# A product-key expert layer: the dense sum over all experts' V rows replaced by gathers of the chosen rows

## What is computed

```python
e = (i1 * PEER_NKEYS + i2).reshape(T, PEER_HEADS * PEER_TOPK)
gate = jax.nn.softmax(cv, axis=-1).reshape(T, PEER_HEADS * PEER_TOPK)
act = jax.nn.gelu(jnp.einsum('ted,td->te', u_tab[e], xb).astype(jnp.float32))
coef = (gate * act).astype(xb.dtype)
return jnp.einsum('te,ted->td', coef, v_tab[e])
```

## Time and profile before

| What | Value |
|---|---|
| median of three runs | 5477.62 us |
| span of the profiled execution | 5473.6 us |
| PE busy | 5015.2 us, 92% of the span |
| DVE busy | 2899.3 us, 53% |
| ACT busy | 1068.2 us, 20% |
| POOL busy | 455.4 us, 8% |
| moved by DMA | 476.12 MB, mean 87 GB/s |

### The profile page before, as it was taken

The page is one execution under the profiler, slowest core; times in us unless marked ns, Lnnn a source line. Parts: engine busy times, 40 slices in busy tenths (PEclk is TensorE's granted clock), DMA queues, the critical chain, the costliest instruction groups (busy, mean ns, idle before and its releaser), DMA issues. The chain is left out here.

```text
span 5473.6 us, 76074 instructions
## 1 busy us (share of the span) xinstructions
PE 5015.2 (92%) x26871; PEld 4496.7 (82%) x26871; DVE 2899.3 (53%) x7212; ACT 1068.2 (20%) x1825; POOL 455.4 (8%) x328
## 2 busy tenths in 40 slices
PE   7999889998798999988887699999999999999996
PEld 6757888884598999988887688888888899889886
DVE  1021733333315999877776566666644444444444
ACT  2111111111311222222222211111111121112111
POOL 0000033430000000000000022222200000000000
PEclk9999589999799999999989899999999999999998
DMA  3100300002222233244445533333321221121122
GB/s 114 39 23 16 129 23 1 1 1 85 96 70 79 100 105 110 77 134 131 136 131 144 154 141 140 142 142 133 141 76 57 72 72 59 61 72 64 56 72 81
DMA packets 450919, 476.12 MB, mean 87 GB/s; under 512 B 311344, under 2 KB 376240, under 8 KB 449328
## 3 DMA queue, kind: packets, MB, share of 16 engines
q1 hardware_dynamic: 136240, 354.12, 18.6%
q10 hardware_dynamic: 307728, 91.43, 6.2%
q0 software_dynamic: 6768, 28.32, 1.4%
HBM read 336.45 MB, written 137.36 MB: 87 GB/s over the span
## 5 line engine op out<-in xcount | busy, mean ns | idle before, releaser
L1752 DVE TENSOR_TENSOR peer_y<-peer_y,stored_pv 128x512 f32<-128x512 f32 x648 | 443.0, 686 | 271.1 <-PE stored_pv L1781 270.3
L1779 PE MATMUL stored_pv<-stored_Vh,stored_Ch 128*128 128x512 f32 x1296 | 505.5, 390 | 33.1 <-DVE stored_Cl L1738 33.1
L1780 PE MATMUL stored_pv<-stored_Vl,stored_Ch 128*128 128x512 f32 x1296 | 505.2, 390 | 0.0
L1781 PE MATMUL stored_pv<-stored_Vh,stored_Cl 128*128 128x512 f32 x1296 | 505.1, 390 | 0.0
L1952 DVE TENSOR_TENSOR peer_y<-peer_y,experts_pv 128x512 f32<-128x512 f32 x504 | 341.8, 687 | 286.1 <-PE experts_pv L1992 286.1
L1975 PE MATMUL experts_pu<-peer_xh,experts_Uh 128*128 128x384 f32 x1344 | 450.5, 335 | 7.0 <-DVE experts_Ul L1918 7.0
L1977 PE MATMUL experts_pu<-peer_xh,experts_Ul 128*128 128x384 f32 x1344 | 450.2, 335 | 0.0
L1976 PE MATMUL experts_pu<-peer_xl,experts_Uh 128*128 128x384 f32 x1344 | 450.2, 335 | 0.0
L1990 PE MATMUL experts_pv<-experts_Vh,experts_Ch 128*128 128x512 f32 x1008 | 396.1, 393 | 15.1 <-DVE peer_y L1952 12.7
L1599 DVE TENSOR_SCALAR gates_scaled<-gates_iota,retrieve_slotT 128x128 f32<-128x128 f32 x1152 | 396.2, 344 | 0.0
L1991 PE MATMUL experts_pv<-experts_Vl,experts_Ch 128*128 128x512 f32 x1008 | 393.7, 391 | 0.0
(11 more groups left out here) (297 smaller groups left out, 9408.9 us busy)
## 6 DMA issues: line engine op xcount, KB each, us to landing
gates<-gates_G ACTq DMA_DIRECT2D x72, 1024.0 KB, 11.0
stored_C<-acts SPq DMA_DIRECT2D x72, 576.0 KB, 3.8
stored_G<-gates SPq DMA_DIRECT2D x72, 576.0 KB, 4.8
stored_Vr<-in_peer_v SPq DMA_DIRECT2D x72, 512.0 KB, 6.4
experts_G<-gates SPq DMA_DIRECT2D x56, 576.0 KB, 3.8
experts_Ur<-in_peer_u SPq DMA_DIRECT2D x56, 512.0 KB, 5.7
experts_Vr<-in_peer_v SPq DMA_DIRECT2D x56, 512.0 KB, 5.9
acts<-topk_act SPq DMA_DIRECT2D x135, 192.0 KB, 1.9
```

The lines of the kernel that those rows point to most:

```text
L1752: nc.vector.tensor_tensor(dst, dst, pv[r % RING][:], ALU.add).then_inc(y_added, 1)
L1779: mm(pv[r % RING][:], Ch[p][j][:, t], Vh[p][j][:, cols], start=(j == 0), stop=False)
L1780: mm(pv[r % RING][:], Ch[p][j][:, t], Vl[p][j][:, cols], start=False, stop=False)
L1781: last = mm(pv[r % RING][:], Cl[p][j][:, t], Vh[p][j][:, cols], start=False, stop=(j == 1))
```

## The change

The Gelu values of all 128 blocks are now made in topk (6 blocks a tile, 54 in all) and in a new stage rest (74 blocks, U products only), and stored to DRAM. They go to nine tensors `acts0` to `acts8`, one per tile of tokens, in which the value of expert e and token t is cell 128 e + t. The stages gates, stored and experts are removed. A new stage values computes from `slotT` the expert number `row` and the cell number `cell` of each token's 128 slots. Per token POOL then issues two indirect DMAs: one brings the 128 Gelu values into a column of `act`, one brings the 128 rows of V (4 KB each) into one of 16 buffers, a row per partition. DVE multiplies the values of a tile by their weights and writes them to a matrix W that is zero elsewhere; PE multiplies W (128 slots x 32 columns, one of which is not zero) by the token's V rows, in plain float32, and sums 32 tokens into 32 partitions of PSUM. Four tokens are handled in turn, each in its own group of 32 columns of the PE array. ACT copies a finished tile to `y`.

The diff, cut to what the prediction speaks of (removed stages are printed above):

```diff
 class Ahead:
     def store(self, sp, n):
         for c in range(NTC):
             sp.wait_ge(self.gelu_done, 3 * n + (c + 4))
-            sp.dma_start(self.dram["acts"][n + self.first][:, c * TC:(c + 1) * TC], self.act[c][:]).then_inc(self.act_out[c], 16)
+            for t in range(TC // P):
+                dst = self.dram[f"cells{c * (TC // P) + t}"][n + self.first]
+                sp.dma_start(dst, self.act[c][:, t * P:(t + 1) * P]).then_inc(self.act_out[c], 16)
...
-TOPK_AHEAD = 5
-GATE_AHEAD = 3
+TOPK_AHEAD = 6
...
-                    if half == 0:
-                        ahead.low(dve, t * A + 4, 4)
+                    ahead.low(dve, t * A + 4 + half, 4 + half)
...
+def stage_rest(core, xh, xl, first):
+    R = 2
+    LEFT = P - first
...
+        def _(sp):
+            ahead.load(sp, 0)
+            with sp.Fori(0, LEFT // R - 1) as i:
+                for b in range(R):
+                    ahead.load(sp, i * R + (b + 1))
+                    ahead.store(sp, i * R + b)
...
+        def _(pe):
+            ahead.begin(pe=pe)
+            with pe.Fori(0, LEFT // R) as i:
+                for b in range(R):
+                    for c in range(NTC):
+                        ahead.products(pe, i * R + b, b, c)
...
+def stage_values(core, y):
+    Q = 4
+    QW = P // Q
+    RING = 16
...
+        def _(pool):
+            def gather_act(i, t):
+                pool.indirect_dma_start(act[i % 2][:, t:t + 1], None, dram[f"acts{i}"],
+                                        bass.IndirectOffsetOnAxis(ap=cell[:, i * P + t:i * P + t + 1], axis=0))\
+                    .then_inc(act_in[i % 2], 16)
+
+            def gather_row(i, m, j):
+                n = (i * QW + m) * Q + j
+                if n >= RING:
+                    pool.wait_ge(v_used, (n - RING) // Q + 1)
+                t = i * P + j * QW + m
+                pool.indirect_dma_start(V[n % RING][:], None, dram["peer_v"],
+                                        bass.IndirectOffsetOnAxis(ap=row[:, t:t + 1], axis=0)).then_inc(v_in[n % RING], 16)
...
+            for t in range(P):
+                gather_act(0, t)
+            pool.wait_ge(rows_made, 1)
+            for i in range(TILES):
+                if i >= 1 and i + 1 < TILES:
+                    pool.wait_ge(coef_done, i)
+                for m in range(QW):
+                    for j in range(Q):
+                        if i + 1 < TILES:
+                            gather_act(i + 1, m * Q + j)
+                        gather_row(i, m, j)
...
+        def _(pe):
+            for i in range(TILES):
+                pe.wait_ge(coef_done, i + 1)
+                if i >= 2:
+                    pe.wait_ge(tile_read, i - 1)
+                for m in range(QW):
+                    n = (i * QW + m) * Q
+                    for half in range(2):
+                        for j in range(Q):
+                            if half == 0:
+                                pe.wait_ge(v_in[(n + j) % RING], 16 * ((n + j) // RING + 1))
+                            last = nc.tensor.matmul(py[i % 2][j * QW:(j + 1) * QW, half, :], W[i % 2][:, j, m * QW:(m + 1) * QW],
+                                                    V[(n + j) % RING][:, half * HW:(half + 1) * HW],
+                                                    start=(m == 0), stop=(m == QW - 1))
+                    last.then_inc(v_used, 1)
...
                 stage_topk(core, xh, xl)
-                stage_gates(core, xh, xl)
+                stage_rest(core, xh, xl, TILES * TOPK_AHEAD)
             y = pr.sb("y", [P, TILES, D])
-            made = TILES * (TOPK_AHEAD + GATE_AHEAD)
-            stage_stored(core, y, made)
-            stage_experts(core, xh, xl, y, made)
+            stage_values(core, y)
             stage_final(core, y)
```

More of the change, by code:

```diff
@@ L1552, in _ @@
             turn(TILES - 1)
-def stage_gates(core, xh, xl):
-    nc, dram = core.nc, core.dram
[L1561 to L1578, removed]
+def stage_rest(core, xh, xl, first):
+    nc = core.nc
+    R = 2
+    LEFT = P - first
+    with Stage(core, "rest") as st:
+        ahead = Ahead(core, st, R, first, xh, xl)
+        block = st.block()
+        @block.sync
+        def _(sp):
[4 more added lines that the diff above has]
+                    ahead.store(sp, i * R + b)
+            ahead.load(sp, LEFT - 1)
+            ahead.store(sp, LEFT - 2)
+            ahead.store(sp, LEFT - 1)
+            ahead.stored(sp, LEFT)
+        @block.scalar
+        def _(act):
+            ahead.begin(act=act)
+            ahead.high(act, 0, 0)
+            with act.Fori(0, LEFT // R - 1) as i:
+                for b in range(R):
+                    ahead.high(act, i * R + (b + 1), (b + 1) % R)
+                    ahead.gelu(act, i * R + b)
+            ahead.high(act, LEFT - 1, 1)
+            ahead.gelu(act, LEFT - 2)
+            ahead.gelu(act, LEFT - 1)
+        @block.vector
+        def _(dve):
+            ahead.begin(dve=dve)
+            with dve.Fori(0, LEFT // R) as i:
+                for b in range(R):
+                    ahead.low(dve, i * R + b, b)
+        @block.tensor
+        def _(pe):
+            ahead.begin(pe=pe)
+            with pe.Fori(0, LEFT // R) as i:
+                for b in range(R):
+                    for c in range(NTC):
+                        ahead.products(pe, i * R + b, b, c)
@@ new lines, in stage_values @@
+def stage_values(core, y):
+    nc, dram = core.nc, core.dram
+    Q = 4
+    QW = P // Q
+    RING = 16
+    with Stage(core, "values") as st:
+        tok = st.sb("tok", [P, TILES, P])
+        expert = st.sb("expert", [P, T])
+        row = st.sb("row", [P, T], U32)
+        cell = st.sb("cell", [P, T], U32)
+        act = [st.sb(f"act{i}", [P, P]) for i in range(2)]
+        W = [st.sb(f"W{i}", [P, Q, QW * QW]) for i in range(2)]
+        V = [st.sb(f"V{i}", [P, D]) for i in range(RING)]
+        py = [st.psum(f"py{i}", [P, 2, HW]) for i in range(2)]
+        tok_done = st.sem("tok_done")
+        w_zero = st.sem("w_zero")
+        ch = st.sem("chain")
+        cells_made, rows_made = st.sem("cells_made"), st.sem("rows_made")
+        act_in = [st.sem(f"act_in{i}") for i in range(2)]
+        v_in = [st.sem(f"v_in{i}") for i in range(RING)]
+        coef_done = st.sem("coef_done")
+        v_used = st.sem("v_used")
+        tile_made = st.sem("tile_made")
+        tile_read = st.sem("tile_read")
@@ L1586, in _ @@
         @block.vector
         def _(dve):
[L1588 to L1600, removed]
+            link = Chain(dve, ch)
@@ L1602, in _ @@
         @block.tensor
         def _(pe):
[L1604 to L1617, removed]
@@ L1619, in _ @@
-        @block.scalar
[L1620 to L1649, removed]
```

349 lines of the change are left out of this document (41 added, 308 removed).

## The result

The changed kernel takes 6659.34 us (median of four runs, 6656.88 to 6660.9) against 5477.17 us before: 1.216 times as long, 95% interval 1.2145 to 1.2179. The forecast of 5897 us had the sign right; the time lies inside the range, close to its upper end, and the loss is 1182 us where 419 us were forecast. The new stage, values, takes some 3260 us in place of 2506 us; everything else came out as summed.

The account below looks back on a forecast made before the run. PE was taken to set the old kernel's pace, and POOL's gathers that of values. 5473.6 - 3133 + 113 + 933, 3391 us against the median, plus 2506 us for values gave 5897 us, 7.7% slower; range 5220 to 6700 us.

Parts of the forecast that it names:

- the sixth block: Topk: a sixth block of U products per tile makes PE the longer side by some 12 us, +113 us over 9 tiles.
- the 74 blocks left over: Rest: 74 blocks at 12.47 us are 923 us, plus 10 us for first load and split, +933 us.
- their cover: Rest: a 7.3 us chain of stores, load and split hides behind a 12.47 us block; 90 us if cover were gone.
- That the gathers decide: Values: POOL's two gathers a token, 2.16 us, are slowest and hide the DMA engines' 1.56 us and PE's 0.43 us.
- the first rival: Values: gathers near the plain 0.54 us, so DMA engines bind at 1.56 us a token; 5277 us, 3.7% faster; chance 0.32.
- The price of a gather: Values: twice a plain DMA's 0.54 us on POOL, 1.08 us for each of 2304 gathers, giving a stage of 2506 us.
- Rival 2: Values: POOL reads index after index or waits for data; 8939 us at 2.4 us a gather; chance 0.10, extreme 0.02 of it.
- Rival 3: Values: PE's column groups run serially, 1.72 us a token; 5462 to 5503 us, or 7512 us at half clock; chances 0.04, 0.03.
- The DMA engines' 1.56 us a token: Values: 1.42 us for a token's V rows plus 0.14 us for its activations, hidden behind POOL's gathers.

Follow-up runs that it names:

- the kernel with the constant tile: Against the changed kernel, PE multiplied a constant tile instead of gathered V rows and POOL waited only for its own earlier landings, not PE's count: 6975.0 us.
- the kernel with nearly nothing else: Against the kernel with the constant tile, PE made only two of the 32 groups of each tile, all gathers kept: 6627.38 us.

## Why the prediction was right or wrong

**Topk and rest: right.** +113 us was forecast and +114 measured for the sixth block; 933 against 936 us for the 74 blocks left over. PE waited in both together for 31 us (21.4 for the first blocks of topk, 9.3 for the first of rest), so the nine small stores in place of three cost nothing, and their cover held.

**That the gathers decide: right, but not as time of POOL.** The DMA engines had time left (share 0.64), PE waited for V, and the first rival (the engines bind) is refuted twice, by rows of 256 B with and without Gelu values. But the gathers do not stand end to end on POOL, as was forecast: it is busy for 1929 of 2891 us, and 758 us of further work on it cost 79 us. Above POOL's own 1.25 us a gather it is a limit behind POOL that binds, which the prediction did not have. Its premise was a gather near the price of a plain DMA. The Trainium skill (DMA: Bandwidth & Descriptors, anatomy of one DMA), which calls descriptor generation small, would lead there; plain DMAs agree (0.54 us in the earlier trace rows, 0.6 us here), gathers do not (0.94 us recorded, 1.40 us in all).

**The price of a gather: wrong, and this is the step that failed.** "So I take it twice: 1.08 us" was to cover writing 128 addresses and reading 128 indices. It missed two things. First, the price on POOL is not the busy time of the record but the distance to the next start: the record is 0.94 us, below the guess, but 0.30 us of issue stand ahead of each, which gives 1.25 us and 2304 x 0.17 = 392 us more. Second, a row of single instructions with time between them can't show a rate that can be kept up: back to back, gathers are held to 1.40 us, another 2304 x 0.15 = 346 us, which show as pauses (378 us). Together 2304 x 0.32 = 737 us of the 754 us by which values came out too long (3260 - 2506). With 1.40 us the sum would have been 3391 + 2304 x 1.40 + 18 = 6635 us, 0.4% below the median. That the time still lies in the range is in part luck: 3258 / 2304 = 1.41 us a gather is just short of the 1.43 us at which the range ends. The unequal shares of indices and bytes that the forecast reasoned with play no part: half the indices in the gathers of Gelu values (64 in place of 128) and a sixteenth of the bytes leave the time within 0.5%, and a gather of 4 B an index is recorded with the same 0.94 us as one of 4 KB.

**Rival 2 (2.4 us a gather, or one operation per index): refuted.** The record is less than half of the time to landing of a plain DMA, and 64 indices fewer save 39 ns.

**Rival 3 (column groups one after another): refuted.** At a granted clock of 1.00 PE made 132 records in 14 us in the kernel with the constant tile, 0.106 us each, where one record of the full array takes 0.43 us: four run at once, and a token's four records take 0.42 us, against 0.43 forecast. The Trainium skill (TensorE: Matmul & The Clock Gate, Part 3, packing small matmuls) gives 2.38 times for three groups, from which 0.6 us a token was estimated; the measurement of four groups, 0.43 / 0.106 = 4.1 times, decides. At the lower level of the clock, where values mostly runs (0.71 on the mean), 34 records took 7.32 us, 0.215 us each; that is hidden as well.

**The DMA engines' 1.56 us a token** could not be seen as a bound anywhere; a share of 0.64 of 2891 / 1024 = 2.82 us is 1.81 us, so the term was low by 0.25 us, at no cost.

No version that beats the kernel before came out of this. The run without Gelu gathers for tiles 1 to 8 took 5246 us, but it leaves out what makes the result, and the 1024 gathers for them cost 1.38 us each.

## What to carry to other kernels

Count indirect DMAs, not their bytes: with 128 indices each costs some 1.40 us here when hundreds follow one another, so gathering one 4 B value per index is as dear as gathering a 4 KB row. Price an instruction by start to start in a long run of it, not by its busy time. And when an engine stalls at a semaphore, lighten the engine that is waited for before you believe it: here the pauses moved from a wait to PE to the gather itself, and the sum per token stayed.

## What was not expected of the hardware

- Gathers back to back keep a limit of their own (1.396 us each over 2006 of them) above POOL's pace of 1.25 us. POOL can run ahead of it for a while: for the first 305 us in the kernel with nearly nothing else, and after a pause in the one with the constant tile it makes 81 gathers in 100 us, and only later 72.
- In the kernel with the constant tile, while they run and some 24 us beyond, 16 us of it with POOL and the DMA engines idle, a PE that waits for no data gets one matmul record through every 2.80 us; its granted clock then reads 0.50, and 1.00 in the stretch in which it makes 132 in 14 us.
- Up to 0.33 us of other work on POOL ahead of each gather is nearly free (79 us of time for 758 us of work), since it falls into time that the gathers lose anyway.
